# A Mamba scan on one core: which of VectorE and ScalarE reads the spread sums first

## What is computed

```python
a_cum = jnp.cumsum(dt * A, axis=2)
...
seg = a_cum[:, :, :, None] - a_cum[:, :, None]
decay = jnp.exp(jnp.where(mask, seg, -jnp.inf))
cb = jnp.einsum('bcign,bcjgn->bcijg', C, B)
y_diag = jnp.einsum('bcijg,bcijgh,bcjghp->bcighp', cb, decay, xdt)
y_off = jnp.einsum('bcign,bcghpn,bcigh->bcighp', C, prev, jnp.exp(a_cum))
return (y_diag + y_off).reshape(b, l, g, hg, p), final
```

## Time and profile before

| | |
|---|---|
| time, median of 3 runs | 2091.94 us (2087.95 to 2092.34) |
| the profiled execution's own time | 2089.19 us |
| its span in the profile | 2087.3 us |
| PE busy | 1944.9 us, 93% of the span |
| DVE busy | 1500.2 us, 72% |
| ACT busy | 1273.6 us, 61% |
| POOL busy | 172.4 us, 8% |
| mean granted TensorE clock | 0.965 of full speed |

### The profile page before, as it was taken

How to read it: one execution, slowest core, us unless ns; L and a number is a source line. 1 busy time by engine, 2 the same in 40 slices (tenths; PEclk the granted TensorE clock), 3 DMA queues, 4 the chain that set the end, 5 groups by cost and what they waited for, 6 DMA issues and landing times.

```text
span 2087.3 us, 30551 instructions
## 1 busy us (share of the span) xinstructions
PE 1944.9 (93%) x11163; PEld 1618.8 (78%) x11164; DVE 1500.2 (72%) x1704; ACT 1273.6 (61%) x1777; POOL 172.4 (8%) x128
## 2 busy tenths in 40 slices
PE   4989889999999888898699999999999999999997
PEld 4967778888877767777587888888888888888885
DVE  2255463223465768778559899898989989898998
ACT  3234473222365445556457888887888888788885
POOL 1000000000000245455100000000000000000100
PEclk8999999999999999999879999999999999999999
DMA  9359723322454212221158999999999999999995
GB/s 329 122 197 380 273 81 101 101 87 95 155 184 150 83 41 81 62 80 61 59 184 318 350 364 377 348 384 355 377 359 365 376 347 386 353 378 357 366 395 196
DMA packets 247202, 503.87 MB, mean 241 GB/s; under 512 B 10347, under 2 KB 62907, under 8 KB 247099
## 3 DMA queue, kind: packets, MB, share of 16 engines
q1 hardware_dynamic: 245952, 499.79, 66.3%
q0 software_dynamic: 576, 2.10, 0.3%
q10 hardware_dynamic: 571, 0.57, 0.1%
HBM read 497.71 MB, written 4.72 MB: 241 GB/s over the span
## 4 chain that ended last, share of the span: by engine, by line
PE 78%; DVE 12%; ACT 5%; DMA 3%; issue 3%; ACTq 0%; SPq 0%; POOL 0%; DVEq 0%
PE bank L775 18%; PE bank L777 18%; PE bank L776 18%; PE bank L1003 4%; PE bank L1005 4%; PE bank L1004 4%; DVE ar L2310 3%; DVE lo L1992 3%; PE bank L1358 1%; PE bank L801 1%; DMA raw<-in_ada_w_dram 1%; PE bank L1078 1%; PE bank L1079 1%; PE bank L1080 1%; PE bank L1333 1%
## 5 line engine op out<-in xcount | busy, mean ns | idle before, releaser
L1992 DVE TENSOR_TENSOR lo<-raw,hi 128x1024 fp32r<-128x1024 f32 x844 | 1031.1, 1239 | 330.8 <-ACT hi L1438 245.5
L1456 ACT ACTIVATE hi<-raw 128x1024 fp32r<-128x1024 f32 x672 | 712.8, 1061 | 183.0 <-PE bank L777 180.7
L775 PE MATMUL bank<-hi,xh_t 128*128 128x512 f32 (+1 forms) x1184 | 451.0, 381 | 26.6 <-DVE lo L1992 15.7
L777 PE MATMUL bank<-hi,xl_t 128*128 128x512 f32 (+1 forms) x1184 | 448.1, 378 | 0.0
L776 PE MATMUL bank<-lo,xh_t 128*128 128x512 f32 (+1 forms) x1184 | 447.9, 378 | 0.0
L1438 ACT ACTIVATE hi<-raw 128x1024 fp32r<-128x1024 f32 x128 | 135.4, 1061 | 288.5 <-PE bank L1005 172.6
L775 PEld LDWEIGHTS bank<-hi,xh_t 128*128 128x128 f32 x1184 | 226.2, 191 | 69.7 <-issue 29.0
L777 PEld LDWEIGHTS bank<-hi,xl_t 128*128 128x128 f32 x1184 | 225.8, 191 | 41.1
L776 PEld LDWEIGHTS bank<-lo,xh_t 128*128 128x128 f32 x1184 | 226.3, 191 | 39.8
L775 PE MATMUL bank<-hi,hth 128*128 128x512 f32 x624 | 249.0, 399 | 3.1 <-DVE lo L1992 3.1
L777 PE MATMUL bank<-hi,htl 128*128 128x512 f32 x624 | 244.0, 391 | 0.0
(11 more groups left out here) (320 smaller groups left out, 2179.4 us busy)
## 6 DMA issues: line engine op xcount, KB each, us to landing
raw<-in_moe_gu_w_dram SPq DMA_DIRECT2D x224, 1024.0 KB, 7.1
raw<-in_moe_down_w_dram SPq DMA_DIRECT2D x112, 1024.0 KB, 7.2
raw<-in_ada_w_dram SPq DMA_DIRECT2D x24, 2048.0 KB, 10.0
raw<-in_ffn_gu_w_dram SPq DMA_DIRECT2D x22, 1024.0 KB, 5.0
raw<-in_ffn_down_w_dram SPq DMA_DIRECT2D x22, 1024.0 KB, 4.9
raw<-in_ssm_in_w_dram SPq DMA_DIRECT2D x16, 1024.0 KB, 5.4
raw<-in_mix_out_w_dram SPq DMA_DIRECT2D x8, 1024.0 KB, 11.4
raw<-in_ssm_out_w_dram SPq DMA_DIRECT2D x8, 1024.0 KB, 5.1
```

The costliest lines, as they stand in the source:

```text
L775: mm(o, a_hi, w_hi, start=first, stop=False, **kw)
L777: return mm(o, a_lo, w_hi, start=False, stop=last, **kw)
L1456: A_(hi[:, p % SPL, :], raw[:, u, (p % 2) * PIECE:(p % 2 + 1) * PIECE], ACT.Copy).then_inc(m_hi, 1)
L1992: TT(lo[:, p % SPL, :], raw[:, u, h * PIECE:(h + 1) * PIECE], hi[:, p % SPL, :].bitcast(F32), ALU.subtract).then_inc(done, 1)
```

## The change

VectorE's maximum takes the bank as soon as TensorE has written it (it waits for `bc_t` and no longer for `ce_exp`), and ScalarE's exponential of the bank waits for the maximum (`sg_ready`) in place of `bc_t`. TensorE may write the bank again when the exponential is done (`ce_exp`) in place of the maximum. The order of the instructions within each engine is the same.

```diff
@@ TensorE, bc(g, q)
                 if n >= 2:
-                    pe.wait_ge(sg_ready, n - 1)
+                    pe.wait_ge(ce_exp, n - 1)
@@ TensorE, behind the last group
-            pe.wait_ge(sg_ready, N_GROUPS * NQ)
+            pe.wait_ge(ce_exp, N_GROUPS * NQ)
@@ ScalarE, ce_(g, q)
-                act.wait_ge(bc_t, n + 1)
+                act.wait_ge(sg_ready, n + 1)
@@ VectorE, seg(g, q)
-                dve.wait_ge(ce_exp, n + 1)
+                dve.wait_ge(bc_t, n + 1)
```

## The result

| | before | changed |
|---|---|---|
| median of 4 runs each, us | 2091.18 | 2068.84 |
| ratio, 95% interval | | 0.9895 (0.9883 to 0.9907) |
| the profiled execution's own time | 2089.19 | 2067.68 |
| its span | 2087.3 | 2065.8 |
| first matmul of the scan, us from the start | 738.77 | 734.65 |

A group is counted from the first matmul of its `bc` (line 1133) to that of the next. In the two profiles the four groups are 19.3 us shorter together. The profiled executions themselves are 21.5 us apart. The other 2.2 us are 4.1 us less ahead of the scan, where nothing was changed, and 1.9 more behind it. The first experiment shows how far the stretch ahead of the scan spreads from one execution to the next.

What follows compares the result with a forecast made beforehand. TensorE's chain ended last for 78%, with some 8 us per full group without a matmul. Gains of 16.2 (full groups), 0 (group 3) and 2 (clock) make 18 us: 2091.94 to 2074, range 2066 to 2086.

Steps and rivals of the forecast that it cites:

- VectorE no longer waits for ScalarE: Full groups, unit 3: `seg(3)` needs only the bank and `yy(1)`, so it and `seg(4)` start 2.9 us earlier.
- ScalarE now waits for VectorE: Full groups, unit 4: `ce_(4)` runs behind `seg(4)`, `m_(4)` comes 2.2 us earlier, PE's gap of 3.80 shrinks by 2.2.
- The second detour: Full groups, unit 5: `seg(5)` 6.3 us earlier, `m_(6)` 5.4 earlier; a full group gains 5.4 us, three of them 16.2.
- GpSimd's multiplication comes later: GpSimd, units 0 and 4: its multiplication starts later, for unit 4 by 3 us, covered by 3.4 us.
- The heads: Slot 0 of each group: `ce_(0)` waits for `seg(0)`; nothing in groups 0 to 2, `state_lat` 4.5 us later in group 3.
- I take 0: Group 3: its end comes between 1 us early and 2 us late, counted as 0.
- The clock: TensorE, slot behind the shortened gaps: if the clock stays up, 1.5 us per full group; between 0 and 4.5, 2 taken.
- A sign of being wrong: Line 1992: the forecast is wrong if GpSimd's casts become what it waits for, or a full group takes over 73 us.
- Rival 1: VectorE's `mul` meets GpSimd more often, up to 1.08 us each, 9.7 us in all, leaving 8: 2084; chance 0.20.
- Rival 2: `seg` really waits for `yy`: nothing arrives but 0.6 us per full group, 1.8 us, 2090; chance 0.08.
- Rival 3: Group heads, `ce_(0)`: ScalarE stands behind VectorE, 4.5 us each in groups 1 to 3, clock lost: 2096; chance 0.06.
- The table load: ScalarE, ahead of the exponential: counted as 1.28 us; with the skill's drain of 1.38 us the sum would be 15.

Runs made afterwards that it cites:

- The first experiment: The kernel before, unchanged, run and profiled once more against the kernel before: ratio 0.9995 (0.9986 to 1.0003), scan starting at 735.75 us.

## Why the prediction was right, and where it was off

- *VectorE no longer waits for ScalarE.* Right in place and size for the maximum: `seg(3)` 2.8 us earlier. Units 3 and 5 alone carry two thirds of the gain, and each carries its own part.
- *ScalarE now waits for VectorE.* The exponential ahead of `m_` costs 0.5 us, against 0.7 priced. `m_(4)` came 2.9 earlier and not 2.2. The other 0.5 are one instruction of `state` between `seg(3)` and `seg(4)`, which took 1.28 us beside GpSimd's multiplication (848.02 to 849.31) before and 0.68 now; taps and `mul` there did not get shorter.

```profile
848.58 1.28 DVE L2376 TENSOR_TENSOR raw<-ar 128x512 f32<-128x512 f32 x1
```

```profile
836.15 0.68 DVE L2376 TENSOR_TENSOR raw<-ar 128x512 f32<-128x512 f32 x1
```

- *The second detour.* I shifted VectorE's queue with its old durations. The taps ahead of `seg(5)` took 6.13 us (4.55 before), those behind it 4.01 (5.45 before), and at `m_(6)` the errors left 6.0 in place of 5.4. The taps of 6.13 us are also behind TensorE's second gap in slot 6, which the forecast did not have. What I had as a mere cover, "GpSimd's multiplication comes later", is worth something of its own, as the runs with GpSimd held show: held back, GpSimd starts behind the maximum.
- *The heads.* Right: covered in full groups, 4.65 us late in group 3. "I take 0" measured +0.25 and -0.05, as the sum of the head's price (2 to 2.8 us with the change, 2.9 without) and what the rest of the group gives back.
- *The clock.* This is the term that was mis-sized. I took 2 of 4.5 us, which was a choice between bounds and not worked out. In all three full groups of both profiles of the changed kernel the clock stayed up in slot 8: its 24 matmuls took 2.95 to 2.99 us, and 4.44 in each full group of the profile before. That is the whole 4.5. About 0.5 us a group of it is lost again behind slot 8, where I had the rest of the group run at TensorE's pace.
- *A sign of being wrong.* "If GpSimd's casts become what line 1992 waits for" came true in a small way, three waits of 0.9 us, one in each full group, at its end. The forecast of a cover of 3.4 us was for the cast of unit 4 alone. The waits belong to the 0.5 us just named; what each would be worth by itself was not measured.
- *Sum.* 18 against 19.3 in the profiles' scans, 21.1 with the start of group 0 alike, and 22.3 in the medians. From 18 to 21.1 it is 2.5 for the clock and 1.8 for VectorE's chain (0.6 a group at `m_(6)`: 0.2 is the cheaper hand-over, and the rest is that VectorE's instructions got no longer in sum, for which I had allowed), less 1.5 behind slot 8. The last 1.2 us are not explained one by one; the second profile of the kernel before, whose scan is 3 us longer than the first's (half of it the start of group 0), shows that the base moves by that much. That 18 lay within 4 us of the medians is thus in part luck: two terms too small and one loss left out.
- *Rival 1*, VectorE meeting GpSimd more often: real as a mechanism (0.68 us become 1.78), wrong in its sign for the whole change (from `seg(3)` to `seg(6)` of group 1 VectorE's own work took 23.89 us, after 24.16), right for the change of two units alone. `mul` grew by 1.1 us beside a multiplication of 1.85. The multiplication ended at 847.42 and `mul` at 847.96, 0.54 us later. The rule of the Trainium skill, "SBUF — State Buffer", section "SBUF: two separate sides", that of a VectorE instruction with two SBUF inputs and a GpSimd instruction that reads SBUF the second is blocked for the whole of the first, fits these rows.
- *Rival 2* is out: the hand-over alone would have given 1.8 us. *Rival 3*: its place was right, but it decides in group 3 alone, where the clock was lost as it says: the two matmuls of `state_lat` behind the wait of 5.29 us took 2.07 us, and 1.13 before.
- *The table load.* In the changed kernel the one at 836.15 takes 1.28 us and its exponential starts at 837.45, 0.02 us after it. The drain of about 1.38 us that the Trainium skill, "ScalarE: Activation LUTs", section "What ACT_TABLE_LOAD costs", adds is not seen here either, nor behind any other load of this trace: behind 31 of its 37 loads the next instruction starts within 0.02 us, and behind the other six ScalarE waits for VectorE.

```profile
836.15 1.28 ACT L1777 ACT_TABLE_LOAD   x1
837.45 0.60 ACT L1777 ACTIVATE ar<-bank 128x512 f32<-128x512 f32 x1
```

## What to carry to other kernels

Where two engines read one buffer in turn, let the one go first whose own queue is the bound, and look for what the other engine has queued ahead of its read: here a SiLU, a copy and a table load stood between VectorE and a bank that had been full for long, 3.4 us twice a group. Check the swap unit by unit, since at places where the first reader is late (the group heads) the old order is better. And a wait that holds a third engine back can pay, if the two engines' instructions lengthen each other, as 0.68 us became 1.78 here. Last, read a gain on the bounding engine twice, as idle time and as busy time: here half of the 7 us of group 1 was TensorE's clock, which no longer fell behind the shorter gaps.

## What was not expected of the hardware

- One added wait on GpSimd gained 2.4 to 2.9 us per full group with units 3 and 5 swapped, and 1.4 with the order as before.
- ScalarE's table load was done ahead of the wait of the instruction it belongs to: loaded by 942.26, waited until 946.71.
- Behind gaps of 1.41 and 1.91 us in slot 6 TensorE's granted clock fell to 0.50 in groups 0 and 2 of one profile of the changed kernel, and held 1.00 in its group 1 and in all three full groups of the other. Behind a gap of 0.92 us or less ahead of slot 8 it never fell in these two.
- At the start of the scan the granted clock rose from 0.50 after some 2.5 us in one execution and some 6 us in another, with the same kernel and the same work, and that moved group 0 by 1.5 us.
